# Two-layer RWKV-7 / sparse-attention encoder on one core: VectorE's modulation halves and the remainder of old heads at other places of the mixing stage

## The chip, the core and the metric

The kernel runs on one core of one Trainium2 chip. The metric is the time of one execution on the device in microseconds. The engines are TensorE (matmul), VectorE, ScalarE, GpSimd and SyncE (SP), which here issues nearly all DMAs.

## What is computed

The program takes x (256 tokens x 2048) and a conditioning vector c through two layers: an RWKV-7 time mixer and a DeepSeek-style sparse attention, each followed by a SwiGLU FFN, each sub-layer under RMSNorm with shift, scale and gate from c, and a final norm. All is float32 (matmuls with operands split in a high and a low part). The change touches the RWKV mixer and the modulation:

```python
mod_all = jnp.einsum('bd,lde->lbe', jax.nn.silu(c), ada_w) + ada_b[:, None, :]   # 2 x 12288 x 2048
...
def step(S, inp):                                # per head, N = 64, over 256 tokens
    r_t, w_t, k_t, v_t, kk_t, a_t = inp
    sa = jnp.einsum('bhij,bhj->bhi', S, -kk_t)
    S = (S * w_t[:, :, None, :] + sa[..., None] * (kk_t * a_t)[:, :, None, :]
         + v_t[..., None] * k_t[:, :, None, :])
    y = jnp.einsum('bhij,bhj->bhi', S, r_t)
    return S, y
...
y = ((y - mean) * lax.rsqrt(var + A_GN_EPS)).reshape(B, T, D) * ln_w + ln_b
y = (y + bonus.reshape(B, T, D)) * g
```

## The kernel before, in words

The stage in question is `rwkv`: 32 heads of 64, two heads to a tile of 128 partitions, two tiles (j = 0, 1) to an iteration, L = 8 iterations (i = 0 to 7). The recurrence is done in four chunks of 64 tokens (NC = 4, c = 0 to 3). Each iteration has three parts, which all engines run in the same order, bound to each other by semaphores (`at(engine, i, name, j)` waits for the step `name` of tile j):

- **stage M**: the products M1, M3, M2 of the chunk's keys; VectorE masks them (XE, Dd, A, BF) and starts W.
- **stage N / W**: the inverse of a 64 x 64 triangular matrix by doubling: TensorE makes DX2, DX4, D8B, P2, P3, P4, TZ16, W32, TZ32, W64; ScalarE takes DX2, DX4, D8B, VK and the TZ; VectorE adds each step to W (`grow`: P2, P3, P4, W32, W64).
- **stage C**: per chunk R (taken by ScalarE), U (taken by VectorE, `Uu`), the state S (ScalarE); behind the last chunk Yp, and M1 of the next iteration.

In between, preparation of iteration i + 1 is done: ScalarE's `prep_v` (q, from the loaded tile `in`, the first thing of stage N, for both j, ahead of DX2), squares, Exp, and in chunk 0 `prep_norm` (Ln, Exp); VectorE's `prep_a` (scan), `prep_b` to `prep_e`. So is the end of iteration i - 1 (`normed`, `gated_in`, `gated`) and `remainder(i - 2)`, which writes the low part of finished heads.

VectorE also computes part of the modulation: 24 tiles of 128 rows of ada_w, as six halves of 128 x 1024 in each iteration (`ada_half`, L1984: a product with silu(c) and a sum into column n of `parts`), and `ada_sums`, two short instructions that add the halves and the bias. The halves' loads go through a ring of three places: half n lies in place n mod 3.

SP issues every DMA of the stage in an order written out by hand. A load of a half waits until the half that had its place is done; with HALVES = 6:

```python
def ada(i, *ns):
    for n in ns:
        if not (isinstance(i, int) and i == 0 and n < 3):
            sp.wait_ge(s("ada_half"), i * HALVES + (n - 2))
        sp.dma_start(place(n), ...).then_inc(s(f"half_loaded{n % 3}"), 16)
def body(i, more):
    ada(i, 4, 5)
    ada(i + 1, 0, 1, 2)
    if more:
        tiles(i + 2)
    gates(i)
    ada(i + 1, 3)
```

`tiles(i)` issues, for each j, once bon, vb and kka of iteration i - 1 are done, two loads of `in` from DRAM scratch: L2000 (384 KB: r, k, v) and L2004 (256 KB: decay and a). They are loaded for i = 2 to 7 in `body(0)` to `body(5)`. `gates` loads g, 2 x 128 KB. A half's load is 512 KB.

Of the kernel before, what the change touches and what calls it, by code (L numbers as in the profile page):

```python
# [1587 lines left out]
class Program:  # L1588
# [22 lines left out]
    def s(self, name):  # L1611

        if name not in self.sems:
            self.sems[name] = self.nc.alloc_semaphore(name)
        return self.sems[name]
# [309 lines left out]
    def rwkv(self, loras):  # L1925
# [14 lines left out]
        def bank(j, b, side=LEFT):  # L1940
            return ps[:, 4 * j + b, side]
# [5 lines left out]
        def heads4(ap):  # L1947
            return ap.rearrange("p (c n) -> p c n", c=NC)
# [18 lines left out]
        def at(eng, i, name, j):  # L1967
            wait(eng, name, i * 2 + (j + 1 + one(name)))
# [12 lines left out]
        def ada_half(dve, i, n):  # L1981

            dve.wait_ge(s(f"half_loaded{n % 3}"), i * 32 + 16 * (n // 3 + 1))
            nc.vector.scalar_tensor_tensor(place(n), place(n), 1.0, self.silu[:, (n % 2) * W:(n % 2 + 1) * W], MUL, MUL,  # L1984
                                           accum_out=self.parts[:, n:n + 1]).then_inc(s("ada_half"), 1)
# [244 lines left out]
        def vector(dve):  # L2230
            def tt(name, out, a, b, op):
                nc.vector.tensor_tensor(out, a, b, op).then_inc(s(name), 1)  # L2232

            def col(i, first, j):
                return self.pv[:, bass.ds(i * 2 + (first + j), 1)]

            def prep_a(i):
                for j in range(2):
                    b = R[j]
                    dve.wait_ge(s(f"in_loaded{j}"), i * 32 + 32)  # L2240
                    past(dve, i, "Pn")
                    nc.vector.tensor_tensor_scan(b["Ls"][:], self.carry[:], b["in"][:, 3, :], 0.0, MUL, ADD).then_inc(s("Ls"), 1)

            def prep_b(i, j):
                b = R[j]
                r, k, v, sw, a = (b["in"][:, n, :] for n in range(5))
                nc.vector.tensor_scalar(b["k2"][:], a, col(i, PV_KA, j), self.omka[:, bass.ds(i * 2 + j, 1)], MUL, ADD).then_inc(s("t1"), 1)
                at(dve, i, "t1", j)
                tt("k2", b["k2"][:], b["k2"][:], k, MUL)
                at(dve, i, "k2", j)  # L2250
                nc.vector.scalar_tensor_tensor(b["rb"][:], r, col(i, PV_RK, j), b["k2"][:], MUL, MUL).then_inc(s("rb"), 1)

            def prep_c(i, q):
                for j in range(2):
                    at(dve, i, "rbs", j)
                    past2(dve, i, "yb")
                    tt("bon", R[j]["bon"][q][:], bank(j, 0, RIGHT), R[j]["in"][:, 2, :], MUL)

            def prep_d(i, j):
                b = R[j]  # L2260
                at(dve, i, "Pn", j)
                past(dve, i, "M2p")
                past(dve, i, "kept")
                tt("rho", b["rho_al"][:, :, 1], chunks(b["in"][:, 0, :]), b["Pi"][:, :, 1:], MUL)
                past(dve, i, "D8Bp")
                tt("ka", b["ka"][:], b["k2"][:], b["Pn"][:], MUL)

            def prep_e(i, j):
                b = R[j]
                at(dve, i, "rkn", j)  # L2270
                tt("kkn", b["kk"][:], b["q1"][:], b["rk"][:], MUL)
                at(dve, i, "kkn", j)
                tt("kka", b["q1"][:], b["kk"][:], b["in"][:, 4, :], MUL)
                tt("al", b["rho_al"][:, :, 0], chunks(b["kk"][:]), b["Pi"][:, :, 0:C], MUL)
                at(dve, i, "kka", j)
                tt("be", b["be"][:], b["q1"][:], b["Pn"][:], MUL)
# [19 lines left out]
            def keys(i):  # L2296
                for j in range(2):
                    at(dve, i, "M2p", j)
                    tt("BF", R[j]["BF"][:], pairs_of(j, 0), bc_pairs(self.m_BF), MUL)

            def normed(i):
                for j in range(2):
                    b = R[j]
                    at(dve, i, "rsv", j)
                    tt("yn", b["y"][:], b["yc"][:], b["yr"][:], MUL)

            def gated_in(i, q):
                for j in range(2):
                    b = R[j]
                    at(dve, i, "yn", j)  # L2310
                    at(dve, i, "bon", j)
                    nc.vector.scalar_tensor_tensor(b["y"][:], b["y"][:], col(i, PV_LNW, j), b["bon"][q][:], MUL, ADD).then_inc(s("yb"), 1)

            def gated(i):
                for j in range(2):
                    b = R[j]
                    at(dve, i, "yb", j)
                    dve.wait_ge(s(f"g_loaded{j}"), i * 16 + 16)
                    nc.vector.scalar_tensor_tensor(b["yo"][:], b["y"][:], col(i, PV_LNB, j), b["g"][:], ADD, MUL).then_inc(s("yg"), 1)

            def remainder(i):
                for j in range(2):
                    at(dve, i, "y_hi", j)
                    m = bass.ds(i * 2 + j, 1)
                    tt("y_lo", self.hid_lo[:, m, :], R[j]["yo"][:].unsqueeze(1), self.hid_hi[:, m, :].bitcast(F32), SUB)

            def grow(i, name, b, op, prev):
                for j in range(2):
                    at(dve, i, name + "p", j)
                    at(dve, i, prev, j)  # L2330
                    tt(name, R[j]["W"][:], R[j]["W"][:], heads4(bank(j, b)), op)

            def adas(i, *ns):
                for n in ns:
                    ada_half(dve, i, n)

            def ada_sums(i):
                parts = self.parts[:, 0:HALVES].rearrange("p (m h) -> p m h", h=2)
                dve.wait_ge(s("ada_half"), i * HALVES + HALVES)
                at = bass.ds(i * TILES + ADA_FIRST, TILES)  # L2340
                tt("halves", self.mod[:, at], parts[:, :, 0], parts[:, :, 1], ADD)
                dve.wait_ge(s("halves"), i + 1)
                tt("mod_ready", self.mod[:, at], self.mod[:, at], self.pv[:, bass.ds(i * TILES + (PV_ADA + ADA_FIRST), TILES)], ADD)

            def stage_N(i, q, post, prep):
                keys(i)
                if prep:
                    prep_a(i + 1)
                adas(i, 2)
                grow(i, "P2", 3, ADD, "P1")  # L2350
                if prep:
                    for j in range(2):
                        prep_b(i + 1, j)
                grow(i, "P3", 3, ADD, "P2")
                grow(i, "P4", 3, ADD, "P3")
                if post:
                    normed(i - 1)
                    gated_in(i - 1, 1 - q)
                grow(i, "W32", 1, SUB, "P4")
                if prep:  # L2360
                    prep_c(i + 1, 1 - q)
                adas(i, 3, 4)
                if i >= 2:
                    remainder(i - 2)
                adas(i, 5)
                grow(i, "W64", 3, SUB, "W32")

            def stage_C(i, post, prep):
                for c in range(NC):
                    for j in range(2):  # L2370
                        dve.wait_ge(s("Up"), i * 8 + (2 * c + j + 1))
                        nc.vector.tensor_copy(R[j]["Uu"][:], bank(j, 3, slice(c * HD, (c + 1) * HD))).then_inc(s("U"), 1)
                    if c == 0:
                        if prep:
                            for j in range(2):
                                prep_d(i + 1, j)
                        ada_sums(i)
                    if c in (1, 2) and prep:
                        prep_e(i + 1, c - 1)
                    if prep and c % 2:  # L2380
                        adas(i + 1, c // 2)
                    if c == 2 and post:
                        gated(i - 1)

            prep_a(0)
            for j in range(2):
# [6 lines left out]
                prep_d(0, j)  # L2393
                prep_e(0, j)
            stage_M(0)
            adas(0, 0, 1)
            stage_N(0, 0, False, True)
            stage_C(0, False, True)
            stage_M(1)
            for i in range(1, L - 2, 2):  # L2400
# [22 lines left out]
        def tensor(pe):  # L2423
# [201 lines left out]
            for u in range(3):  # L2625
                pe.wait_ge(self.s("unit_split"), s0 + u + 1)
                pe.wait_ge(s("y_lo"), UK * (u + 1))
                self.multiply(u, UK, UK * u, KT, COLS, ((0, P), (P, 2 * P)), self.hid, (0, 1)).then_inc(self.s("unit_used"), 1)

        return Stage(sync, scalar, vector, tensor)  # L2630

    def ffn(self, layer, pieces, following):
# [119 lines left out]
```

## Time and profile before

| | us |
|---|---|
| median of 3 runs (2628.6 to 2630.26) | 2628.8 |
| the profiled execution | 2628.9 |
| its span in the profile | 2627.3 |
| TensorE matmul busy | 2526.0 (96%) |
| VectorE busy | 1899.0 (72%) |
| ScalarE busy | 1253.8 (48%) |
| mean granted TensorE clock | 0.987 |

The span is the time from the first to the last instruction in the profile; 1.6 us of the execution lie outside. Most of the kernel is dense matmul. The mixing stage is the part from about 395 to 680 us, where many short instructions of three engines follow one another. In the rows below, a line of the timeline is: start, duration of the group, engine, line, operation, output<-input and shape, count, and in brackets the idle time before it and what ended it. "x2" is a group of two that follow directly; its duration runs to the end of the second. The next instruction of an engine may start a little before the one ahead has ended. L2431 is the helper of all small matmuls, L2232 that of VectorE's tensor_tensor, L2046 that of ScalarE's copies.

### The profile page before, as it was taken

Reading aid. Unit: us, or ns where it says so; the run is one execution under the profiler, and the core shown is the slowest. Engines: PE = TensorE matmul, PEld = TensorE weight load, DVE = VectorE, ACT = ScalarE, POOL = GpSimd, SP = SyncE. Lnnn points to the kernel's source line nnn. Section 1 sums busy time; section 2 is a strip of 40 time slices with the busy share of each in tenths; the row PEclk is TensorE's granted clock in tenths of the full one; section 3 lists DMA queues with packets and bytes.
Section 4 is the critical chain, followed back from the end, with each engine's and each line's share of the span. In section 5 each row is a group of like instructions: output and inputs, shape, how many; then the busy total and the mean of one; then the engine's idle time right before and its main releaser. Section 6 shows DMA issues by size and latency. Waiting matters only on the chain.

```text
span 2627.3 us, 53443 instructions
## 1 busy us (share of the span) xinstructions
PE 2526.0 (96%) x20124; PEld 2223.5 (85%) x20124; DVE 1899.0 (72%) x2596; ACT 1253.8 (48%) x1926; POOL 46.5 (2%) x85
## 2 busy tenths in 40 slices
PE   7999997998899999999999999999999999999998
PEld 6888877888788888888888888888888888888887
DVE  6868757887687777777777776677887655555556
ACT  2245555666445444444444554344454444444445
POOL 2000020000000000000000000000000000000000
PEclk9999999999999999999999999999999999999999
DMA  9998893445568888888887678567688566656653
GB/s 401 416 319 310 288 336 118 145 142 182 192 232 273 285 295 282 285 287 285 283 286 266 218 237 285 186 218 244 236 295 286 195 191 190 189 190 191 189 166 133
DMA packets 442249, 640.28 MB, mean 244 GB/s; under 512 B 21920, under 2 KB 402976, under 8 KB 420256
## 3 DMA queue, kind: packets, MB, share of 16 engines
q1 hardware_dynamic: 438400, 626.35, 70.1%
q0 software_dynamic: 3744, 12.59, 1.2%
q8 instruction: 59, 0.97, 0.1%
q14 instruction: 46, 0.38, 0.0%
HBM read 624.18 MB, written 14.68 MB: 243 GB/s over the span
## 4 chain that ended last, share of the span: by engine, by line
PE 68%; DVE 4%; ACT 1%; issue 1%; DMA 0%; DVEq 0%; ACTq 0%; SPq 0%
PE ps L1813 44%; PE ps L1817 22%; DVE ada_ring L1859 1%; DVE wlo L1797 1%; ACT whi L1792 0%; PE ps L1444 0%; PE ps L1438 0%; DMA ada_ring<-in_ada 0%; DVE st L1345 0%; PE ps L1477 0%; PE ps L1835 0%; DVE nt L132 0%; DVE lgf L1342 0%; PE ps L1469 0%; PE ps L1459 0%
## 5 line engine op out<-in xcount | busy, mean ns | idle before, releaser
L1797 DVE TENSOR_TENSOR wlo<-raw,whi 128x1024 fp32r<-128x1024 f32 (+1 forms) x736 | 865.6, 1191 | 436.5 <-ACT whi L1792 435.1
L1813 PE MATMUL ps<-act,whi 128*128 128x512 f32 x3528 | 1095.4, 392 | 0.8 <-DVE act L145 0.8
L1792 ACT ACTIVATE whi<-raw 128x1024 fp32r<-128x1024 f32 (+1 forms) x736 | 745.7, 1030 | 634.6 <-PE ps L1817 628.1
L1817 PEld LDWEIGHTS ps<-act,wlo 128*128 128x128 f32 x3528 | 662.6, 188 | 145.9
L1817 PE MATMUL ps<-act,wlo 128*128 128x256 f32 x3528 | 696.2, 279 | 0.0
L1813 PE MATMUL ps<-hid,whi 128*128 128x512 f32 x2176 | 685.4, 396 | 8.1 <-DVE wlo L1797 7.1
L1813 PEld LDWEIGHTS ps<-act,whi 128*128 128x128 f32 x3528 | 534.9, 188 | 1.4 <-DVE wlo L1797 1.0
L1817 PEld LDWEIGHTS ps<-hid,wlo 128*128 128x128 f32 x2176 | 411.3, 189 | 92.4
L1817 PE MATMUL ps<-hid,wlo 128*128 128x256 f32 x2176 | 433.4, 280 | 0.0
L1813 PEld LDWEIGHTS ps<-hid,whi 128*128 128x128 f32 x2176 | 331.5, 189 | 11.0 <-DVE wlo L1797 4.6
L1859 DVE SCALAR_TENSOR_TENSOR ada_ring<-ada_ring,silu 128x2048 f32<-128x2048 f32 x128 | 292.5, 2285 | 12.8 <-DMA ada_ring<-in_ada 12.8
L1153 PE MATMUL ps<-first_mix,raw 128*128 (+1 forms) x512 | 114.5, 385 | 8.2 <-DVE first_mix L1027 8.2
L1153 PEld LDWEIGHTS ps<-first_mix,raw 128*128 128x128 f32 x512 | 97.6, 192 | 25.1 <-issue 6.9
L94 ACT ACTIVATE small<-ps 128x512 f32<-128x512 f32 x164 | 95.3, 581 | 27.9 <-PE ps L1817 27.9
L391 ACT ACTIVATE hid<-hf 128x512 f32 (+1 forms) x44 | 27.8, 632 | 139.6 <-DVE hf L405 139.6
L388 ACT ACTIVATE sig<-sgt 128x512 f32<-128x512 f32 x44 | 27.8, 632 | 80.5 <-DVE sgt L99 80.5
L408 DVE TENSOR_TENSOR hid<-hf,hid 128x512 f32 (+1 forms) x44 | 30.5, 693 | 44.6 <-ACT hid L391 44.6
L315 ACT ACTIVATE tmp<-x 128x512 f32 (+1 forms) x28 | 17.7, 632 | 92.2 <-DVE x L332 92.2
L332 DVE SCALAR_TENSOR_TENSOR x<-gsum,mod,x 128x256 f32 (+1 forms) x120 | 52.9, 482 | 12.1 <-DVE gsum L99 11.5
L2046 ACT ACTIVATE DX<-ps 128x512 f32<-128x512 f32 x64 | 38.0, 596 | 44.7 <-PE ps L2431 44.5
L1984 DVE SCALAR_TENSOR_TENSOR ada_ring<-ada_ring,silu 128x1024 f32<-128x1024 f32 x48 | 57.5, 1214 | 0.0
L2232 DVE TENSOR_TENSOR W<-W,ps 128x256 f32<-128x256 f32 x80 | 31.9, 418 | 34.7 <-PE ps L2431 33.8
(276 smaller groups left out, 2118.4 us busy)
## 6 DMA issues: line engine op xcount, KB each, us to landing
raw<-in_f_w SPq DMA_DIRECT2D x480, 512.0 KB, 4.5
ada_ring<-in_ada SPq DMA_DIRECT2D x144, 1024.0 KB, 7.7
raw<-in_a_w_rkv SPq DMA_DIRECT2D x96, 512.0 KB, 7.7
raw<-in_b_w_in SPq DMA_DIRECT2D x56, 512.0 KB, 3.8
ada_ring<-in_ada SPq DMA_DIRECT2D x48, 512.0 KB, 5.1
raw<-in_f_w SPq DMA_DIRECT2D x64, 384.0 KB, 3.9
first_ring<-in_ada SPq DMA_DIRECT2D x16, 1024.0 KB, 12.7
raw<-in_a_w_o SPq DMA_DIRECT2D x32, 512.0 KB, 6.8
```

What stands on the lines that cost most here:

```text
L94: p.nc.scalar.activation(self.small[:, g], p.ps[:, 2 * g:2 * g + 2, T:2 * T], ACT.Copy).then_inc(p.s(f"small_out{g}"), 1)
L332: last = p.nc.vector.scalar_tensor_tensor(p.x[:, bass.ds(m, 1), :], p.gsum[:, g, b:b + 1, :], p.mod[:, bass.ds(m + 16 * self.gate, 1)], p. ...
L408: nc.vector.tensor_tensor(p.hid_lo[:, bass.ds(i * 2, 2), :], p.hf[:], p.hid_hi[:, bass.ds(i * 2, 2), :].bitcast(F32), SUB).then_inc(s("hid ...
L1153: last = nc.tensor.matmul(p.ps[:, 4 * h + m // 2, (m % 2) * T:(m % 2 + 1) * T], p.raw[:, u, m * P:(m + 1) * P], src[:, bass.ds(k, 1), :].r ...
L1792: self.nc.scalar.activation(self.whi[:, u % SPL, 0:n], self.raw[:, u, 0:n], ACT.Copy).then_inc(self.s("hi_ready"), 1)
L1797: self.nc.vector.tensor_tensor(self.wlo[:, u % SPL, 0:n], self.raw[:, u, 0:n], self.whi[:, u % SPL, 0:n].bitcast(F32), SUB).then_inc(self. ...
L1813: self.nc.tensor.matmul(self.ps[0:c1 - c0, banks[b], :], hi[:, kk, c0:c1], src[:, k].rearrange("p a t -> p (a t)"), start=k == 0, stop=False)
L1817: last = self.nc.tensor.matmul(self.ps[0:c1 - c0, banks[b], T:2 * T], lo[:, kk, c0:c1], src[:, k, 0, :], start=False, stop=k == ktotal - 1)
L1859: self.nc.vector.scalar_tensor_tensor(tile, tile, 1.0, self.silu[:], MUL, MUL, accum_out=self.mod[:, bass.ds(r * 2 + (a + j), 1)]).then_in ...
L1984: nc.vector.scalar_tensor_tensor(place(n), place(n), 1.0, self.silu[:, (n % 2) * W:(n % 2 + 1) * W], MUL, MUL, accum_out=self.parts[:, n:n ...
L2046: nc.scalar.activation(dst, src, ACT.Copy, scale=scale).then_inc(s(name), 1)
L2232: nc.vector.tensor_tensor(out, a, b, op).then_inc(s(name), 1)
```

## The change

VectorE's order in stages N and C is changed; no instruction is added or taken away, and SP, ScalarE and TensorE keep their code. In stage N half 1 stands where half 2 was, half 2 ahead of W32, and behind W32 only half 3 is left. In stage C `remainder` stands in chunk 0, half 4 in chunk 1, and half 5, `ada_sums` and half 0 of the next iteration behind the last U (chunk 3). Before, chunk 0 had `ada_sums`, chunk 1 half 0 and chunk 3 half 1 of the next iteration.

```diff
@@ stage_N
                 keys(i)
                 if prep:
                     prep_a(i + 1)
-                adas(i, 2)
+                adas(i, 1)
                 grow(i, "P2", 3, ADD, "P1")
@@
                 if post:
                     normed(i - 1)
                     gated_in(i - 1, 1 - q)
+                adas(i, 2)
                 grow(i, "W32", 1, SUB, "P4")
                 if prep:
                     prep_c(i + 1, 1 - q)
-                adas(i, 3, 4)
-                if i >= 2:
-                    remainder(i - 2)
-                adas(i, 5)
+                adas(i, 3)
                 grow(i, "W64", 3, SUB, "W32")
@@ stage_C
                         if prep:
                             for j in range(2):
                                 prep_d(i + 1, j)
-                        ada_sums(i)
+                        if i >= 2:
+                            remainder(i - 2)
                     if c in (1, 2) and prep:
                         prep_e(i + 1, c - 1)
-                    if prep and c % 2:
-                        adas(i + 1, c // 2)
+                    if c == 1:
+                        adas(i, 4)
                     if c == 2 and post:
                         gated(i - 1)
+                    if c == 3:
+                        adas(i, 5)
+                        ada_sums(i)
+                        if prep:
+                            adas(i + 1, 0)
@@ before the first stage_N
-            adas(0, 0, 1)
+            adas(0, 0)
```

## Rows read from the trace of the kernel before

**Rows 1.** The page's costliest groups: busy, mean ns, idle before.

```profile
L1984 DVE SCALAR_TENSOR_TENSOR ada_ring<-ada_ring,silu 128x1024 f32<-128x1024 f32 x48 | 57.5, 1214 | 0.0
```

**Rows 2.** Windows (PE, PEld, DVE, ACT, POOL busy, clock, DMA, GB/s): iterations 2, 5, 6.

```profile
469.80:503.20 33.40, 30.24 (x922) 28.66 (x916) 28.74 (x73) 22.16 (x60) 0.00 (x0) 0.95 0.44 144
...
569.60:602.00 32.40, 29.20 (x921) 27.60 (x915) 28.74 (x73) 22.21 (x61) 0.00 (x0) 1.00 0.47 146
602.00:635.10 33.10, 30.33 (x912) 28.71 (x908) 28.67 (x72) 22.06 (x59) 0.00 (x0) 0.95 0.53 176
...
626.00:627.00 1.00, 1.00 (x25) 1.00 (x23) 0.61 (x4) 0.45 (x2) 0.00 (x0) 0.50 0.64 234
```

**Rows 3.** Timeline of VectorE, W32 to W64 of iteration 6.

```profile
617.81 0.89 DVE L2232 TENSOR_TENSOR W<-W,ps 128x256 f32<-128x256 f32 x2 [1.67 <-PE ps L2431]
618.62 0.75 DVE L2232 TENSOR_TENSOR bon<-ps,in 128x256 f32<-128x256 f32 x2
619.28 1.22 DVE L1984 SCALAR_TENSOR_TENSOR ada_ring<-ada_ring,silu 128x1024 f32<-128x1024 f32 x1
...
621.57 0.76 DVE L2232 TENSOR_TENSOR hid<-yo,hid 128x256 fp32r<-128x256 f32 x2
622.24 1.22 DVE L1984 SCALAR_TENSOR_TENSOR ada_ring<-ada_ring,silu 128x1024 f32<-128x1024 f32 x1
...
623.38 0.75 DVE L2232 TENSOR_TENSOR W<-W,ps 128x256 f32<-128x256 f32 x2
```

**Rows 4.** Timeline of TensorE, the first U product of iteration 6.

```profile
621.84 0.31 PE L2431 MATMUL ps<-BF,VK 64*64 64x64 f32 x4
624.04 0.33 PE L2431 MATMUL ps<-Rr,W 64*64 64x64 f32 x4 [1.89 <-DVE W L2232]
```

**Rows 5.** Timeline of TensorE, the same place in iterations 0, 1 and 7.

```profile
421.15 0.33 PE L2431 MATMUL ps<-Rr,W 64*64 64x64 f32 x4 [1.17 <-DVE W L2232]
...
459.51 0.33 PE L2431 MATMUL ps<-Rr,W 64*64 64x64 f32 x4 [1.22 <-DVE W L2232]
...
659.98 0.33 PE L2431 MATMUL ps<-Rr,W 64*64 64x64 f32 x4 [0.96 <-DVE W L2232]
```

**Rows 6.** Timeline of ScalarE, R to S of iteration 6.

```profile
621.85 0.45 ACT L2046 ACTIVATE Rr<-ps 128x64 f32<-128x64 f32 x2
...
623.00 0.89 ACT L2089 ACTIVATE rk<-rk,cst 128x256 f32<-128x256 f32 x2
625.15 0.32 ACT L2192 ACTIVATE S<-ps,Pi_end 128x64 f32<-128x64 f32 x1 [1.26 <-PE ps L2431]
```

**Rows 7.** Timeline of VectorE, from the last U of iteration 5 on.

```profile
600.05 0.47 DVE L2372 COPY Uu<-ps 128x64 f32<-128x64 f32 x2
600.44 1.22 DVE L1984 SCALAR_TENSOR_TENSOR ada_ring<-ada_ring,silu 128x1024 f32<-128x1024 f32 x1
...
601.95 0.69 DVE L2232 TENSOR_TENSOR XE<-ps,m_XE 128x512 f32<-128x512 f32 x1 [0.28 <-PE ps L2431]
```

**Rows 8.** Timeline of SP's queue, the tile loads of j = 1, iteration 5.

```profile
598.92 0.37 SPq L2000 DMA_DIRECT2D in<-scr  x1
599.48 0.37 SPq L2004 DMA_DIRECT2D in<-scr  x1
```

**Rows 9.** Landing: the L2004 load at 599.48; the weight loads at 636.2 (L1777).

```profile
DMA to landing us min/median/max: 3.5/3.5/3.5
...
DMA to landing us min/median/max: 8.7/8.7/8.7
```

**Rows 10.** Timeline of ScalarE and TensorE, start of stage N of iteration 6.

```profile
602.63 0.91 ACT L2056 ACTIVATE q<-in,pv 128x256 f32<-128x256 f32 x2
...
604.26 0.60 ACT L2046 ACTIVATE DX<-ps 128x512 f32<-128x512 f32 x1 [0.72 <-PE ps L2431]
...
605.89 2.06 PE L2431 MATMUL ps<-DX 64*64 64x64 f32 x64
```

**Rows 11.** Timeline of ScalarE, DX2 of iteration 1.

```profile
438.31 0.60 ACT L2046 ACTIVATE DX<-ps 128x512 f32<-128x512 f32 x1 [2.76 <-PE ps L2431]
```

## The prediction

> **What bounds the kernel now.** I read the page's groups first [rows 1]: the modulation halves, 48 of 1.21 us, are 57.5 us of VectorE work, so it matters where they lie, not that they exist. Then the granted clock and busy time by iteration: a steady pair of head tiles takes 32.4 us at full TensorE clock and 33.1 to 33.4 us where the clock is at half (1.2 instead of 2.4 GHz) for a while [rows 2]; there are eight iterations, the whole stretch is 395 to 680 us, and what follows it (the output projection) can't begin earlier, so a microsecond gained or lost here counts in full. Within an iteration the timelines show a relay: TensorE multiplies, ScalarE or VectorE takes the result, TensorE goes on. Whoever is late stops all.
>
> The place that the change is aimed at is the step W64. Behind W32 VectorE does bon, half 3, half 4, the remainder and half 5, and only then W64, at 623.38 [rows 3]. TensorE has had its last work at 621.84 and stands 1.89 us, released by VectorE's W [rows 4]. That is the largest TensorE wait of a steady iteration. In iterations 1, 0 and 7 the same wait is 1.22, 1.17 and 0.96 us [rows 5].
>
> **Part 1: three steps leave the way of W64.** A half takes 1.14 us of VectorE's queue (622.24 to 623.38), the remainder 0.67 (621.57 to 622.24) [rows 3]. Behind W32 now stand only bon and half 3, which end at 620.42 (619.28 + 1.14). W64 can then start when its product is there, about 621.1, and the next bound is ScalarE's R, whose two copies start at 621.85 [rows 6]: first done about 622.1, and the first U product starts 0.2 us later, at 622.3 instead of 624.04. That is 1.74 us earlier. But ScalarE's next jobs are the Ln and Exp of prep_norm until about 623.8 (623.00 + two of 0.4), and only then can it take S, which would be wanted at 625.15 - 1.74 = 623.4 [rows 6]. S gates the next chunk, so about 0.4 us come back: 1.35 us gained in iterations 2 to 6. Iterations 0 and 1 have the smaller waits and the same ScalarE jobs: 0.65 and 0.7. Iteration 7 has no preparation: 0.9. Sum 5 x 1.35 + 0.65 + 0.7 + 0.9 = **9.0 us gained**; at the most 11 (no S effect), at the least 7 (the wait of 1.2 us and less is partly something else).
>
> **Part 2: half 2 goes in front of W32, half 1 behind the keys.** VectorE waits 1.67 us for TensorE before W32 [rows 3]; 1.14 fits. If that cover were gone, 1.14 us an iteration. Half 1 takes the place that half 2 had. Both zero. In chunk 0 the remainder (0.67) replaces the two short sums (about 0.3); VectorE gets there earlier by the gain of part 1, so zero, at most 0.4 an iteration. Half 4 takes half 0's slot in chunk 1: zero.
>
> **Part 3: behind the last U.** Today one half stands there (600.44 to 601.58) and XE is released by TensorE at 601.95 [rows 7]. With half 5, the sums (0.3) and half 0 of the next iteration XE starts at 600.44 + 1.14 + 0.3 + 1.14 + 0.1 = 603.1, 1.15 us late, and VectorE has no idle time from there to the third W step, so that would all be paid. This alone would cost 7 x 1.1 = 7.7 us and leave the change at a small gain. It isn't what ends last, though.
>
> **Part 4: SP's queue, which the diff does not touch.** SP issues in order: halves 4, 5, then halves 0, 1, 2 of the next iteration, then `tiles(i+2)`, then the gates. The load of half 2 of iteration i+1 goes into the place of half 5 of iteration i and waits until that half is done. Today it is done before W64, some 9 us before the tiles are wanted. After the change it is done behind the last U, and the four tile loads stand behind this wait. They are what ScalarE's first step of stage N (prep_v, for both j) and VectorE's scan wait for, and ScalarE takes DX2 only after prep_v.
>
> Take t = the time at which VectorE is through with the last U (600.44 in the traced boundary). Before: the last tile load is issued at 599.48 = t - 1.0 [rows 8], lands 3.5 us later [rows 9] at t + 2.5, and prep_v's second half runs from about t + 2.6 (602.63, two of 0.4 each): already without slack. DX2 is taken at t + 3.8, and its product DX4 starts at t + 5.4 [rows 10]. After: half 5 done at t + 1.2; SP issues half 2's load at t + 1.4 (0.17 us lag); then four tile loads at 0.58 us each (598.92, 599.48 [rows 8]), the last at t + 3.7. The bounds for its landing: with 3.5 us as now, t + 7.2; at the pace of the burst of four weight loads of 512 KB behind one half, where the last took 8.7 us [rows 9], which is 2560 KB in 10.7 us, the 1792 KB here would take 7.5 us, t + 8.9. I take t + 8.0, nearer to the middle since the queue is empty at its start. Then prep_v's second (0.5), DX2 (0.6) and the lag (0.15) put DX4's product at t + 9.25 instead of t + 5.4: **3.8 us lost** at each boundary (3.0 to 4.75). XE's delay of part 3 lies within this. Everything behind (P2, D8B, P3, P4) is as tight as now, so it is not won back.
>
> The Trainium skill bears on this. "DMA: Bandwidth & Descriptors", section "Rules for kernel authors", says to issue a DMA early and wait for it late; the change does the reverse to the tiles. The same page ("Anatomy of one DMA") gives about 2.0 us plus the bytes at 436 GB/s, by which the burst would land 6.1 us after its first issue, t + 7.5; by this the loss would be 3.3 instead of 3.8. The row of 8.7 us speaks for more.
>
> Tiles 2 to 7 are loaded so: six boundaries. At the first (iteration 0 to 1) DX2 is taken only at 438.31 today because other waits stand there [rows 11], and t + 8.5 is 439.0: zero there, up to 3.8 if those waits shift along. Five boundaries: 5 x 3.8 = 19.0. The last boundary (6 to 7) has no tiles, so part 3's 1.1 is paid.
>
> **The clock.** Half clock is granted behind the W64 wait, in chunks 0 and 1 (626 to 627: 0.50 [rows 2]), in iterations 2, 3, 4 and 6, at 0.7 to 1.0 us each (33.1 to 33.4 against 32.4). That wait goes, but TensorE gets a new one of some 2.6 us in stage N (its work ahead of DX4 ends at 605.89 = t + 5.45 today [rows 10], with XE's delay at t + 6.6, and DX4 starts at t + 9.25), denser with matmuls behind it. I take it at 1.2 us in five iterations against 4 x 0.85 today: + 2.6; from - 3.4 (none) to + 5.
>
> **Sum**, against the profiled execution (2628.9 us, span 2627.3; the median is 2628.8): 19.0 + 1.1 + 2.6 - 9.0 = + 13.7: **2642 us**, 0.5% slower.
>
> **Rivals.**
> A. The tile loads are not decisive: they would have to land by about t + 3.3. Then only part 3 counts: - 9.0 + 7 x 1.1 = - 1.3, and with no half clock - 4.7: 2624 to 2628. For it: the W64 wait is real and released by VectorE. Against: the wait for half 5 stands in front of the tiles in the code, and prep_v has no slack. Chance 0.08.
> B. Cheap wait: landing at t + 7.2, full 11 us gain, no half clock: 5 x 3.05 + 1.1 - 11 - 0 to - 3.4 = + 2 to + 5: 2631 to 2634. Chance 0.08.
> C. Dear wait: landing at t + 8.9, 2 us at the first boundary too, + 5 for the clock, gain only 7: 5 x 4.75 + 2 + 1.1 - 7 + 5 = + 25: 2654. Point of decision: whether the half load's 512 KB hold the tiles up as the weights do. Chance 0.12.
> Forecast 0.72, on its own 2635 to 2650.
>
> **Numbers.** About 0.2% (5.3 us) is what can be told from no change. Faster by more: only A's lower end, 0.05. Within: the rest of A and most of B, 0.08. Slower: 0.87. Range 2633 to 2655: it leaves out A and some of B, 0.12 together, and little of C.
>
> **What would show it.** Right: tile loads issued about 1.9 us and more behind the half that follows the last U, ScalarE's q waiting for a DMA of `in`, 3 to 5 us, in stage N of iterations 2 to 6; TensorE idle before DX products; no idle time before U's first product; a period of 35 to 37 us. Wrong: the loads issued in chunk 2 as now, XE released by VectorE alone and no DMA wait on ScalarE; a period of 33 us or less.

## The result, and the profile after

The changed kernel takes 2658.4 us (median of 5 runs, 2654.8 to 2661.9) against 2628.8 for the kernel before: ratio 1.0118, 95% interval 1.0107 to 1.0129. It is 29.6 us slower. The profiled execution has a span of 2656.6 us against 2627.3, so the 29.3 us of the two traces are what has to be explained. The forecast was 2642, at most 2655: the direction is right, the loss came out at twice its size.

First the windows from XE to XE of iterations 5 and 6 (columns as in [rows 2]). They take 38.2 and 38.0 us where the same iterations took 32.4 and 33.1 before [rows 2]; VectorE is busy only 0.5 to 0.6 us more in them and ScalarE 0.2 us less. The last line is a stretch within stage N of iteration 5: the half clock is granted there now.

```profile
590.40:628.60 38.20, 31.40 (x914) 29.33 (x904) 29.33 (x75) 21.99 (x59) 0.00 (x0) 0.96 0.38 124
628.60:666.60 38.00, 31.03 (x912) 28.96 (x904) 29.20 (x73) 21.89 (x59) 0.00 (x0) 0.96 0.55 179
...
600.00:601.00 1.00, 1.00 (x24) 1.00 (x22) 0.00 (x0) 0.72 (x3) 0.00 (x0) 0.50 0.29 66
```

VectorE's timeline behind the last U of iteration 4 answers to [rows 7]. With t = 587.76, XE starts at t + 2.68 instead of t + 1.51, and has no idle time before it: VectorE itself is what releases it.

```profile
587.76 1.22 DVE L1984 SCALAR_TENSOR_TENSOR ada_ring<-ada_ring,silu 128x1024 f32<-128x1024 f32 x1
...
589.02 0.16 DVE L2232 TENSOR_TENSOR mod<-parts 128x3 f32<-128x3 f32 x1
...
589.29 1.22 DVE L1984 SCALAR_TENSOR_TENSOR ada_ring<-ada_ring,silu 128x1024 f32<-128x1024 f32 x1
...
590.44 0.69 DVE L2232 TENSOR_TENSOR XE<-ps,m_XE 128x512 f32<-128x512 f32 x1
```

SP's queue at the same boundary, against [rows 8]: the last tile load goes out at 591.71 = t + 3.95, where it was t - 1.0.

```profile
589.85 0.38 SPq L2000 DMA_DIRECT2D in<-scr  x1
590.42 0.38 SPq L2004 DMA_DIRECT2D in<-scr  x1
591.14 0.37 SPq L2000 DMA_DIRECT2D in<-scr  x1
591.71 0.37 SPq L2004 DMA_DIRECT2D in<-scr  x1
```

ScalarE and TensorE at the start of stage N, against [rows 10]. q waits 5.60 and then 1.52 us for a DMA; DX2 follows it at once; TensorE stands 4.31 us, released by ScalarE's DX, and starts DX4 at 598.87 = t + 11.1 instead of t + 5.45. The 64 products of DX4 then take 3.50 us instead of 2.06.

```profile
595.57 0.51 ACT L2056 ACTIVATE q<-in,pv 128x256 f32<-128x256 f32 x1 [5.60 <-DMA in<-scr]
597.60 0.51 ACT L2056 ACTIVATE q<-in,pv 128x256 f32<-128x256 f32 x1 [1.52 <-DMA in<-scr]
598.13 1.08 ACT L2046 ACTIVATE DX<-ps 128x512 f32<-128x512 f32 x2
...
598.87 3.50 PE L2435 MATMUL ps<-DX 64*64 64x64 f32 x64 [4.31 <-ACT DX L2046]
```

The wait of [rows 4] is gone, as intended. The first U product has no idle time of note before it, and the next bound is the one foreseen: S comes straight behind prep_norm's Exp and TensorE waits for it.

```profile
616.77 0.33 PE L2435 MATMUL ps<-Rr,W 64*64 64x64 f32 x4
618.79 0.33 PE L2435 MATMUL ps<-S,rho_al_kept 64*64 64x64 f32 x4 [0.28 <-ACT S L2192]
```

Over 470 to 636 us the groups of waits (who waited for whom: us, times, longest) put the new one on top:

```profile
ACT q L2056 <- DMA in<-scr: 36.3, 10, 5.9
...
PE ps L2435 <- ACT DX L2046: 17.6, 4, 4.8
...
DVE Ls L2242 <- DMA in<-scr: 7.6, 7, 1.7
PE ps L2435 <- DVE Dd L2232: 4.8, 5, 1.0
```

I cut each iteration into three stretches: from t (VectorE through with the last U) to DX4's product, from there to the first U product, and from there to the next t. Sums over iterations 2 to 6, from the timelines:

| stretch | before | after | difference |
|---|---|---|---|
| t to DX4 | 27.3 | 56.1 | + 28.8 |
| DX4 to U | 90.8 | 90.3 | - 0.5 |
| U to next t | 47.2 | 45.6 | - 1.6 |

The rest, up to the last U each time: + 1.0 ahead of the stage, + 0.6 in iteration 0, + 2.0 in iteration 1, and - 1.0 from the last U of iteration 6 to the end of the kernel. With the 26.7 of the table that makes 29.3.

### The profile page after: what moved, and what is told of

Same layout as the page of the kernel before. It is cut to its first block, busy times and chain, and to the rows that moved or that the text cites. A ratio compares the mean times of both kernels' runs of the same rounds, so it can differ in the third digit from the quotient of the medians.

```text
span 2656.6 us, 53443 instructions
## 1 busy us (share of the span) xinstructions
PE 2534.0 (95%) x20124; PEld 2229.1 (84%) x20124; DVE 1901.9 (72%) x2596; ACT 1252.0 (47%) x1926; POOL 46.6 (2%) x85
## 4 chain that ended last, share of the span: by engine, by line
PE 67%; DVE 4%; ACT 1%; issue 1%; DMA 0%; DVEq 0%; ACTq 0%; SPq 0%
PE ps L1813 43%; PE ps L1817 22%; DVE ada_ring L1859 1%; DVE wlo L1797 1%; ACT whi L1792 0%; DVE nt L132 0%; PE ps L1444 0%; PE ps L1438 0%; DVE act L145 0%; DMA ada_ring<-in_ada 0%; DVE st L1345 0%; PE ps L1477 0%; DVE lgf L1342 0%; PE ps L1469 0%; PE ps L1459 0%
## 5 line engine op out<-in xcount | busy, mean ns | idle before, releaser
L2435 PE MATMUL ps<-DX 64*64 64x64 f32 x1280 | 54.8, 246 | 25.5 <-ACT DX L2046 23.5
L2435 PEld LDWEIGHTS ps<-DX 64*64 64x64 f32 x1280 | 51.4, 159 | 28.0 <-issue 27.4
L315 ACT ACTIVATE tmp<-x 128x512 f32 (+1 forms) x28 | 17.7, 632 | 91.9 <-DVE x L332 91.9
```

What stands on the lines that cost most here:

```text
L2435: last = nc.tensor.matmul(o[H[h ^ turned]], lhsT[H[h]], rhs[H[h]], start=start, stop=stop, skip_group_check=True)
```

## The experiments

The theory is that SP's queue makes the loss: the tile loads stand behind the load of half 2, and that waits for half 5, which VectorE now does behind the last U. The rival is that VectorE's three steps behind the last U, which delay XE, make it.

**e1: the tiles ahead of half 2's load** (changed kernel, SP's order alone).

```diff
-    ada(i + 1, 0, 1, 2)
+    ada(i + 1, 0, 1)
     if more:
         tiles(i + 2)
+    ada(i + 1, 2)
```

> The changed kernel with one line of SP's order moved: the tile loads go ahead of the load of half 2 of the next iteration, so they no longer stand behind the wait for half 5. VectorE's order is that of the change. If the tiles' place in SP's queue is the cause, they are issued in chunk 2 again, ScalarE's q doesn't wait for them, and only XE's 1.15 us at seven boundaries stands against the gain at W64: 2624 to 2630 us, XE to XE about 33 us. If VectorE's three steps behind the last U are the cause, nothing changes: about 2658 us, 38 us.

Measured: 2627.6 us, ratio 1.0004 (0.9993 to 1.0015). One step earlier in SP's queue takes away the whole loss; XE to XE is 32.3 to 32.9 us, and XE is as late as in the changed kernel (t + 2.68). The rival falls. One part of the expectation doesn't hold: q still waits for the tiles, though shorter:

```profile
535.88 0.51 ACT L2057 ACTIVATE q<-in,pv 128x256 f32<-128x256 f32 x1 [1.52 <-DMA in<-scr]
537.86 0.51 ACT L2057 ACTIVATE q<-in,pv 128x256 f32<-128x256 f32 x1 [1.48 <-DMA in<-scr]
```

The last load goes out at t - 0.11, and is waited for until t + 5.7. That is 5.8 us for a load that took 3.5 in [rows 9].

**e2: the wait alone, in the kernel before.** VectorE's order is untouched.

```diff
-    ada(i + 1, 0, 1, 2)
+    ada(i + 1, 0, 1)
     if more:
+        sp.wait_ge(s("ada_half"), i * HALVES + (HALVES + 2))
+    ada(i + 1, 2)
+    if more:
         tiles(i + 2)
```

> The kernel before, VectorE's order untouched; SP waits for half 1 of the next iteration (the one behind the last U) ahead of half 2's load and the tiles, so that they are issued as late as in the changed kernel. If SP's queue is the cause, this alone makes the loss, and without the gain at W64: 2655 to 2665 us, with tiles landing 9 to 10 us behind the last U. If VectorE's order is the cause, it stays within 5 us of 2629.

Measured: 2669.7 us, ratio 1.0163 (1.0144 to 1.0182), 5 us above the upper end expected. The cause, put alone into the kernel before, makes the loss and more: XE is on time (t + 1.5), q is waited for until t + 9.5 to 10.3, TensorE waits 5.1 to 5.9 us for DX, and the 1.89 us ahead of U are still there. The mean granted clock of its run is 0.981 against 0.987. TensorE's wait for DX in iteration 4:

```profile
566.31 3.44 PE L2434 MATMUL ps<-DX 64*64 64x64 f32 x64 [5.91 <-ACT DX L2049]
```

**e3: late as before, but ahead of the 512 KB.** The changed kernel; SP waits for half 5, then issues the tiles, then half 2's load.

```diff
-    ada(i + 1, 0, 1, 2)
+    ada(i + 1, 0, 1)
     if more:
+        sp.wait_ge(s("ada_half"), i * HALVES + HALVES)
         tiles(i + 2)
+    ada(i + 1, 2)
```

> The changed kernel; SP still waits for half 5 ahead of the tiles, but issues them ahead of half 2's load of 512 KB. If that load holds the tiles up, their last one lands some 2.5 us earlier (7.0 to 7.5 us behind the last U instead of 9.8): 2643 to 2648 us. If only the late issue counts and the 512 KB go beside, only the 0.55 us of one issue are won: 2655 us.

Measured: 2645.6 us, ratio 1.0075 (1.0054 to 1.0096). The last tile goes out at t + 3.4 (0.5 us earlier) and is waited for until t + 8.2 to 9.2, on the mean 1.3 us earlier than in the changed kernel (8.6 against 9.94), where 2.5 were expected. DX4 starts at t + 9.5 to 10.4 instead of 11.2. The time lies in the range expected although the landing doesn't, because the clock gave something back as well: in two of these iterations (2 and 4) no half clock is granted and the stretch from DX4 to U takes 16.35 us; in the three others it takes 17.9, as in the changed kernel.

**e7: half 2's load at 32 KB instead of 512.**

```diff
-    sp.dma_start(place(n), view[...])
+    w = 64 if n == 2 and not (isinstance(i, int) and i == 0) else W
+    sp.dma_start(place(n)[:, 0:w], view[... , (n % 2) * W:(n % 2) * W + w])
```

> The changed kernel; the load of half 2, which stands ahead of the tiles, brings 64 of its 1024 columns (32 KB instead of 512 KB), from iteration 1 on; its wait and its issue stay. Part of half 2's data is left out, so the modulation of those rows isn't that of the reference. If the 512 KB hold up the tiles, their last lands 1.4 us or more earlier than 9.8 us behind the last U: about 2648 us. If the late issue and the four loads among themselves make the landing, it stays near 2656.

Measured: 2650.5 us, ratio 1.0088 (1.0072 to 1.0103). With the wait and the issue as in the changed kernel, q starts at t + 8.9 to 9.3, so the 512 KB are worth 0.9 us, less than the 1.4 expected, and four tile loads on top of each other take 5.0 us from the last issue. Part of the 8 us by which this kernel is faster is again the clock, which stays full in iteration 6. That is what [rows 9]'s 3.5 us did not show.

**e6: the tiles ahead of the loads of halves 1 and 2.**

```diff
-    ada(i + 1, 0, 1, 2)
+    ada(i + 1, 0)
     if more:
         tiles(i + 2)
+    ada(i + 1, 1, 2)
```

> The changed kernel's VectorE order; SP issues the tiles ahead of the loads of halves 1 and 2 (e1: ahead of half 2 only, behind half 1's, which waits for chunk 1's half). The last tile goes out at t - 1.0 as in the kernel before, the first on its own. If the loads' company explains e1's landing at t + 5.6, DX4 is now held only by XE's 1.15 us, at t + 6.6, 0.3 to 0.8 us earlier than in e1: 2624 to 2627 us, on a level with before. If it doesn't, as e1, 2627.6.

Measured: 2622.1 us, ratio 0.9981 (0.9970 to 0.9992): better than forecast, and faster than the kernel before. The last load goes out at t - 0.96 as before the change and lands 3.3 to 3.6 us later in four of five iterations, in which q doesn't wait for it. DX4 starts at t + 6.61 throughout, XE's delay of 1.16 us and nothing else. Over these five boundaries that is 2.1 us less than in e1; the medians differ by 5.5 us, but the two profiled executions by 0.6 only (2621.7 against 2622.3), so the rest of the 5.5 is not explained. This is the VectorE order of the change without SP's wait, at full clock:

```profile
534.20:566.20 32.00, 29.41 (x908) 27.55 (x904) 28.82 (x73) 21.81 (x59) 0.00 (x0) 1.00 0.45 144
```

**e9 and e10: who stands behind the wait.** In e9 ScalarE's q and square stand behind DX2, DX4 and VK; in e10 VectorE's scan also stands behind half 1 and P2. SP's order is that of the changed kernel, so the tiles are as late.

```diff
 # e9, ScalarE, stage_N
-    if prep:
-        prep_v(i + 1)
     evac(i, "DX2", "DX2", 2)
-    if prep:
-        prep_square(i + 1)
     if post:
         centred_square(i - 1)
     evac(i, "DX4", "DX4", 2)
     evac(i, "VK", "VK", 1)
+    if prep:
+        prep_v(i + 1)
+        prep_square(i + 1)
 # e10, VectorE, stage_N as well
-    if prep:
-        prep_a(i + 1)
     adas(i, 1)
     grow(i, "P2", 3, ADD, "P1")
     if prep:
+        prep_a(i + 1)
```

> The changed kernel, tiles as late as in it; only ScalarE's order in stage N is other: q and its square (the steps that wait for the tiles) stand behind DX2, DX4 and VK instead of ahead of them. If the loss is made by what is queued behind ScalarE's waiting q, DX4 starts at t + 6.6 (XE's delay) instead of t + 11.2, and what is left is VectorE's scan, which waits for the same tiles ahead of P2: P2 2 to 3 us late, XE to XE 34 to 35.5 us, 2636 to 2645 us. If late tiles cost their time wherever they are waited for, it stays at 2656 to 2660 us.

> As e9, and VectorE's scan stands behind half 1 and P2 instead of ahead of them. Then nothing of the matrix chain is queued behind a wait for the tiles at t + 9.9. If the two waits are the whole loss, XE to XE is that of e6, about 32.1 to 33 us: 2622 to 2630 us, although the tiles are as late as in the changed kernel. If the late tiles hold the chain in another way, over 2640 us.

Measured: e9 2632.2 us, 1.0021 (1.0012 to 1.0031), some 4 us better than the lower end expected; e10 2627.9 us, 1.0002 (0.9993 to 1.0012). In both the last tile still goes out at t + 3.95, and DX4 starts at t + 6.61. So the lateness by itself costs nothing that the traces show: it costs what is queued behind the instructions that wait for it, above all ScalarE's DX2. In e9 one wait for the tiles is left, in VectorE's queue (here over 470 to 636 us); in e10 none is:

```profile
DVE Ls L2241 <- DMA in<-scr: 7.6, 8, 1.3
```

From DX4 to U e9 takes 17.8 to 18.5 us and e10 17.2 against 16.34 in e6. In e10 this is the price of moving the steps: q and its square now stand ahead of D8B, and TensorE waits 1.0 us for it in each iteration, a wait that e6 doesn't have (five in e10 over 470 to 636 us):

```profile
PE ps L2433 <- ACT D8B L2046: 5.0, 5, 1.0
```

**e4 and e5: halves spread over the gaps.** In e4 VectorE does the remainder between P3 and P4, half 4 in chunk 0, half 5 and the sums in chunk 1, and behind the last U only half 0. SP's order is the old one. e5 adds e1's order of SP.

```diff
 # e4, VectorE, against the changed kernel
     grow(i, "P3", 3, ADD, "P2")
+    if i >= 2:
+        remainder(i - 2)
     grow(i, "P4", 3, ADD, "P3")
@@ stage_C
     if c == 0:
-        if i >= 2:
-            remainder(i - 2)
+        adas(i, 4)
     if c == 1:
-        adas(i, 4)
+        adas(i, 5)
+        ada_sums(i)
     if c == 3:
-        adas(i, 5)
-        ada_sums(i)
         if prep:
             adas(i + 1, 0)
```

> The changed kernel with VectorE's steps behind the last U spread: the remainder between P3 and P4 (0.6 us idle there before), half 4 in chunk 0, half 5 and the sums in chunk 1, so only half 0 is left behind the last U. Half 5 is then done before chunk 2 and SP's order is harmless as it stands. If the queue and XE's delay are the whole loss, the gain at W64 of 9 us shows: 2618 to 2624 us. If chunks 0 and 1 have no room for it, 2625 to 2630 us.

> The spread order of e4 on VectorE, and in SP's order the tile loads ahead of half 2's load, as in e1. In e4 the loads of half 2 and of four tiles go out within 2.6 us, and the last tile lands 5.3 to 5.9 us behind the last U, so that DX4 starts at t + 6.6 to 7.2 instead of t + 5.45. With half 2's load behind them the first tile goes out in chunk 1, on its own, and lands early. If the burst is what holds e4, DX4 starts at t + 5.5 and 1.2 to 1.7 us are won at six boundaries: 2615 to 2619 us. If chunks 0 and 1 hold it, it stays at 2624.

Measured: e4 2624.2 us, 0.9987 (0.9977 to 0.9996), at the edge of its expectation. XE is on time, but half 2's load and four tiles go out within 2.6 us, q is waited for until t + 5.3 to 5.9, and DX4 starts at t + 6.6 to 7.2. From U to t it takes 9.6 us where the changed kernel takes 9.13, so the halves in chunks 0 and 1 cost 0.4 us an iteration. e5: **2616.3 us, 0.9957 (0.9944 to 0.9971)**, the fastest of all and within its expectation. DX4 starts at t + 5.45 to 5.5, and five iterations in a row take 31.35 us at full clock, XE released by TensorE again:

```profile
498.40:529.70 31.30, 29.43 (x915) 27.56 (x910) 28.69 (x72) 21.95 (x59) 0.00 (x0) 1.00 0.48 149
...
529.71 0.69 DVE L2233 TENSOR_TENSOR XE<-ps,m_XE 128x512 f32<-128x512 f32 x1 [0.28 <-PE ps L2436]
```

**e8: the changed kernel once more.**

> The changed kernel once more, for a second trace. Iteration 0 took 41.0 us in its trace and 39.2 in that of before, 39.3 to 41.2 in the others with the same VectorE order up to there, with idle times of TensorE that nothing releases. If that is chance, iteration 0 comes out elsewhere between 37 and 41 us here, while iterations 2 to 6 repeat 38.0 to 39.4.

Measured once: 2659.2 us. Iterations 2 to 6 take 38.1 to 39.4 us again, iteration 0 takes 40.3. Over all traces of this study iteration 0 lies between 37.0 and 41.2 us, also where nothing in its order differs (39.2 in the kernel before, 41.2 in e2), with TensorE idle for nothing that the profile shows. In the changed kernel:

```profile
398.70 0.62 PE L2435 MATMUL ps<-Dd,XE 64*64 64x64 f32 x14 [2.52 <-issue]
408.30 1.13 PE L2435 MATMUL ps<-minus,be 64*64 64x64 f32 x32 [3.50 <-issue]
```

So a difference of 2 us between two traces in iteration 0 tells nothing about the change. What these waits are was not tried.

## Why the prediction was right in kind and short in size

**Part 1, the gain at W64: right.** At full clock the stretch from DX4 to U takes 16.34 us in e6 against 18.16 before: 1.82 gained where 1.74 was worked out. U to t takes 9.13 us against 8.72 at full clock in iteration 5 before, so 0.41 come back, where 0.4 was said; S starts 1.58 us behind the first U product instead of 1.11. Net 1.41 against 1.35.

**Part 2, nothing for halves 1 and 2: right.** VectorE still waits for TensorE ahead of W32, 0.53 us at 612.37, where 0.53 was left of 1.67.

**Part 3, XE late by 1.15: right,** 1.16 at DX4 (6.61 against 5.45) wherever the tiles don't decide: in iteration 7 of the changed kernel, in e6, e9 and e10.

**Part 4, SP's queue: right as the mechanism** (e1, e2), **wrong in the term for the landing.** This is the step that failed. The prediction took t + 8.0 and as the far bound t + 8.9; in iterations 2 to 6 q's second half starts between t + 9.7 and t + 10.3. What follows it took what was said (1.27 us from there to DX4, 1.25 worked out). Three things were mis-sized. The 3.5 us of [rows 9], the near bound, are those of two loads on their own; four in a row need 5.0 from the last issue (e7), so the near bound could not be had by issuing four at once. The 512 KB ahead add 0.9 (changed kernel against e7). And the last goes out at t + 3.95, not 3.7, since SP spends 0.69 us and not 0.58 from half 2's load to the first tile load, and 0.72 from one tile's second load to the next one's first. 1792 KB took from t + 1.4 to t + 9.8, 213 KB a microsecond, slower than the 239 of the weight loads' burst that served as far bound; why these loads are slower among themselves was not tried. Five boundaries at 5.75 are 28.8 us instead of 19.0: that is 9.8 of the 15.6 us that were missing between the 13.7 worked out and the 29.3 of the two traces. The period came out at 38.0 to 39.4 us where 35 to 37 was said. The remark that half 5 is done "some 9 us before the tiles are wanted" is off, though no term rests on it: in iteration 5 it is done at 591.06, 8.4 us before the last tile load goes out and 11.6 us before q starts.

The page "DMA: Bandwidth & Descriptors" of the Trainium skill (section "Anatomy of one DMA") gives its formula for a single DMA, and for one issued from GpSimd. The estimate that the prediction made by it for five loads of SP was t + 7.5; the trace disagrees by 2.3 us, and the row decides. The page's rule in "Rules for kernel authors", to issue early and wait late, is borne out by e1.

**The clock: right sign, price short.** In stage N half clock costs 1.4 to 1.6 us (DX4 to U 17.7 to 17.9 in the changed kernel against 16.34 in e6), and 2.7 in iteration 3, where it lasted twice as long; 1.2 was taken. In stage C before the change it cost 0.86 in iteration 6 (9.58 against 8.72), where 0.85 was taken. In iterations 2 to 6 this took back 8.6 of the 5 x 1.82 = 9.1 us that the stretch from DX4 to U had gained; 6.0 had been reckoned, so 2.6 more of the missing. The half clock was granted around the end of each of TensorE's waits of 4.2 to 4.8 us (from 599.1 us on in the trace above, where the wait ended at 598.9). The kernels in which TensorE has no wait longer than 1.51 us (e1, e4, e5, e6, e9, e10) show it nowhere in iterations 2 to 6.

**First boundary and the ends:** zero was taken at the first, + 1.5 came (DX4 at t + 12.3 against 10.8). The 1.0 us ahead of the stage and what iteration 0 lost lie within what these parts differ by from trace to trace, and so the gains of 0.65 and 0.7 us worked out for iterations 0 and 1 can't be seen either, though the waits ahead of U are gone there too (0.06 us left). From the last U of iteration 6 on, - 1.0 came where + 0.2 (XE's 1.1 less 0.9) was reckoned. Here the clock was luck: behind U iteration 7 takes 9.6 us at full clock in this trace, 11.3 in the kernel before and 11.1 in e8, both at 0.85.

Of the 15.6 us that were missing, the landing is thus 9.8 and the clock in stage N 2.6; 3.8 lie outside iterations 2 to 6, and only the 1.5 at the first boundary can be named there. The other terms together took off 0.5.

Of the rivals, A's mechanism (the tiles not decisive) is what e6 shows once SP's order is mended: 2622, where 2624 to 2628 was worked out. C, the dear wait, with its own point of decision (whether the half's load holds the tiles up), is nearest to what happened; its price was still short by 4 us, and its landing, t + 8.9, by 0.8 to 1.4.

## What to carry to other kernels

When a step that frees a buffer is moved, follow the buffer to the queue that refills it, and read what stands behind that refill: here the lines moved on VectorE cost 1.2 us an iteration themselves (XE) and gained 1.4 at W64, and the wait of five loads in another engine's queue cost 5.8. Size such a wait by loads in the same company as they will have, not by one that landed alone. And where a late arrival can't be avoided, move the instruction that waits for it behind the work that doesn't need it (e9, e10), which gave back 26 and 30 of the 36 us that lie between the changed kernel and e6.

## What the runs showed of the hardware

Tile loads of 384 and 256 KB from one queue land 3.3 to 3.6 us after the last issue when the pair before goes out 2.3 us or more ahead (the kernel before, and four of five iterations of e6; 3.5 to 4.4 in e5), 4.9 to 5.2 us when the four are issued within 1.9 us (e7), and 5.7 to 6.3 us with 512 KB directly ahead (the changed kernel). In iterations 2 to 6 TensorE's clock fell to half (0.50 granted, 1.2 GHz) during or directly behind each wait of 4.2 to 5.9 us (the changed kernel, e2, e8). Behind the waits of 2.6 to 3.7 us of e3 and e7 it fell in seven of ten iterations, and not in order of their length: it fell after 2.64 us (e3) and stayed full after 3.34 (e7). In the changed kernel the work that follows such a wait pays 1.4 to 1.6 us for it, once 2.7.
